# Delta-rule decays from rows of running sums instead of products with a triangle

## The reference, cut to what matters

```python
gc = jnp.cumsum(g, axis=-1)
diff = gc[..., :, None] - gc[..., None, :]
decay = masked_exp(causal, diff)
a_mat = jnp.where(strict, einsum('bhnid,bhnjd->bhnij', kb, k) * decay, 0.0)
attn = jnp.einsum('bhnid,bhnjd->bhnij', q, k) * decay
...
mu = jnp.mean(o, axis=-1, keepdims=True)
var = jnp.mean(jnp.square(o - mu), axis=-1, keepdims=True)
o = (o - mu) * lax.rsqrt(var + EPS)
```

## Time and profile before

| what | value |
| --- | --- |
| median of 3 runs (lowest to highest) | 2910.33 us (2908.55 to 2910.94) |
| profiled execution, its span | 2911.19 us, 2909.4 us |
| mean granted clock of TensorE | 0.997 |
| TensorE busy | 2861.8 us, 98% of the span |
| VectorE, ScalarE, GpSimd busy | 2027.7 us (70%), 1557.9 us (54%), 418.4 us (14%) |
| chain that ended last | TensorE 63%, issue 27%, VectorE 5%, ScalarE 2%, DMA 1% |
| a slot's load of 512 KB, issue to landing | 4.0 us |

### The profile page before, as it was taken

One profiled execution on the slowest core, in us unless ns is written; L12 is line 12 of the kernel. 1 busy time (PEld: TensorE's weight loads), 2 busy tenths in 40 slices (PEclk: granted clock), 3 DMA queues, 4 the chain that ended last, 5 costly groups with the idle time before them and its releaser, 6 DMA issues.

```text
span 2909.4 us, 44265 instructions
## 1 busy us (share of the span) xinstructions
PE 2861.8 (98%) x16572; PEld 2496.3 (86%) x16572; DVE 2027.7 (70%) x3257; ACT 1557.9 (54%) x2353; POOL 418.4 (14%) x637
## 2 busy tenths in 40 slices
PE   7999999999999999999999999999999999999998
PEld 6899889988988888888888899889988888888887
DVE  6888888888875555545568888888888754555554
ACT  6566656665664444444556556655665644444443
POOL 3222132212200000000011232123211000000000
PEclk9999999999999999999999999999999999999999
DMA  6676677667766666666656766676667666666655
GB/s 162 152 178 166 175 178 176 168 172 178 179 175 198 193 193 195 192 193 187 191 129 171 179 171 171 174 181 171 174 174 177 185 192 194 195 189 196 194 181 166
DMA packets 636358, 521.41 MB, mean 179 GB/s; under 512 B 26480, under 2 KB 504496, under 8 KB 635760
## 3 DMA queue, kind: packets, MB, share of 16 engines
q1 hardware_dynamic: 612944, 483.46, 59.1%
q0 software_dynamic: 22816, 34.00, 6.8%
q10 hardware_dynamic: 384, 1.11, 0.1%
HBM read 487.02 MB, written 2.10 MB: 168 GB/s over the span
## 4 chain that ended last, share of the span: by engine, by line
PE 63%; issue 27%; DVE 5%; ACT 2%; DVEq 2%; POOL 1%; DMA 1%; ACTq 0%; POOLq 0%
PE PJ L1807 41%; PE S L1807 16%; PE RA L1807 3%; PE GB L1807 2%; DVE w_lo L1222 1%; DVE mix L1374 1%; POOL gnorm L592 0%; POOL w_lo L507 0%; DVE region L1409 0%; ACT w_lo L656 0%; DVE region L1412 0%; DVE region L1411 0%; DVEq L1413 0%; DVE region L1419 0%; DVEq L1420 0%
## 5 line engine op out<-in xcount | busy, mean ns | idle before, releaser
L1222 DVE TENSOR_TENSOR w_lo<-raw_w,w_hi 128x1024 fp32r<-128x1024 f32 (+1 forms) x912 | 1055.9, 1160 | 689.1 <-ACT w_hi L658 656.9
L658 ACT ACTIVATE w_hi<-raw_w 128x1024 fp32r<-128x1024 f32 x912 | 963.9, 1058 | 804.7 <-PE PJ L1807 358.2
L1807 PE MATMUL PJ<-h_parts,w_hi 128*128 128x256 f32 (+1 forms) x3840 | 943.7, 327 | 1.6 <-DMA w_lo<-raw_w 1.6
L1807 PE MATMUL PJ<-w_hi,h_parts 128*128 128x512 f32 x2304 | 748.9, 396 | 2.0 <-DVE h_parts L1711 2.0
L1807 PE MATMUL PJ<-h_parts,w_lo 128*128 128x256 f32 x2560 | 721.0, 282 | 0.0
L1807 PEld LDWEIGHTS PJ<-h_parts,w_hi 128*128 128x128 f32 x3840 | 641.2, 191 | 62.0 <-issue 7.9
L1807 PEld LDWEIGHTS PJ<-w_hi,h_parts 128*128 128x128 f32 x2304 | 433.6, 188 | 90.3 <-DVE h_parts L1711 2.4
L1807 PEld LDWEIGHTS PJ<-h_parts,w_lo 128*128 128x128 f32 x2560 | 488.3, 191 | 0.0
L1807 PE MATMUL PJ<-w_lo,h_parts 128*128 128x512 f32 x1152 | 449.7, 390 | 0.0
L1807 PE MATMUL S<-w_hi,h_parts 128*128 128x512 f32 x1152 | 368.4, 389 | 0.0
L1807 PEld LDWEIGHTS S<-w_hi,h_parts 128*128 128x128 f32 x1152 | 216.2, 188 | 45.0
(11 more groups left out here) (377 smaller groups left out, 3449.1 us busy)
## 6 DMA issues: line engine op xcount, KB each, us to landing
raw_w<-w_in SPq DMA_DIRECT2D x576, 512.0 KB, 4.0
raw_w<-w_in SPq DMA_DIRECT2D x512, 128.0 KB, 2.7
raw_w<-w_branch SPq DMA_DIRECT2D x128, 512.0 KB, 4.4
raw_w<-w_out SPq DMA_DIRECT2D x64, 512.0 KB, 4.3
w_lo<-raw_w POOLq DMA_DIRECT2D x112, 256.0 KB, 4.2
raw_w<-s_glu_w SPq DMA_DIRECT2D x16, 512.0 KB, 4.4
ret_decay<-c_ret POOLq DMA_DIRECT2D x16, 128.0 KB, 4.0
out<-x_tok SPq DMA_DIRECT2D x4, 512.0 KB, 4.0
```

The source lines that it names most:

```text
L658: A_(w_hi[i % RING][:, :, :], raw_w[i % RING][:, :, :], ACT.Copy).then_inc(hi_ready, 1)
L1222: TT(w_lo[i % RING][:, 0:ks, :], raw_w[i % RING][:, 0:ks, :], w_hi[i % RING][:, 0:ks, :].bitcast(f32), ALU.subtract).then_inc(raw_used[i % ...
L1807: return nc.tensor.matmul(o, w, m, start=start, stop=stop)
```

## The change

`g_wide[:, a]` is g of the block's tokens spread over 128 columns. Its product with `upto` puts the running sum `gc[j]` along the row of every partition. VectorE then makes the exponents of both forms from this row and the column `gc[i]`, which the kernel already had in `unit_cols`, clamped at 0 on the side that the mask will remove: `dec_t` gets min(row - col, 0), `dec_s` gets max(row - col, 0), negated inside ScalarE's exponential. Two products per unit stand in for five, two Exps for three (one of them over all 384 columns of `dec_t`), and five VectorE operations are new. `dec_s` is now waited for by a semaphore of its own. On VectorE `decay_logs` and `ret_normalize` come ahead of `s5_turn(0)`; on ScalarE both Exps stand where `decays_s` stood (with u = 0 where `decays_t` stood); on GpSimd the retention's power comes ahead of the masking.

```diff
-GA_N, GB_N, HA_N, RA_N, SA_N = 20, 4, 11, 3, 4
+GA_N, GB_N, HA_N, RA_N, SA_N = 20, 3, 11, 3, 4
...
-        g_later = in_work(2, P)
-        g_bc = sq[:, 2, :]
+        g_wide = in_work(2, P)
...
                     if u == 0:
...
+                    else:
+                        pool.wait_ge(r_var_ready, n1 - 1)
+                        nc.gpsimd.tensor_tensor(r_rs[:, :], r_rs[:, :], mhalf[:, 0:2], ALU.pow).then_inc(r_rs_ready, 1)
                     pool.wait_ge(dec_raised, n1)
                     nc.gpsimd.tensor_tensor(dec_t[:, 0:3:2, :], dec_t[:, 0:3:2, :],
                                             upto.unsqueeze(1).to_broadcast([P, 2, P]), ALU.mult).then_inc(dec_masked, 1)
-                    if u:
-                        pool.wait_ge(r_var_ready, n1 - 1)
-                        nc.gpsimd.tensor_tensor(r_rs[:, :], r_rs[:, :], mhalf[:, 0:2], ALU.pow).then_inc(r_rs_ready, 1)
...
                     for a in range(2):
-                        A_(g_later[:, a, :], after, ACT.Copy, scale=gate_g[:, a, ds(v, 1)])
-                    A_(g_bc, ones[:, :], ACT.Copy, scale=gate_g[:, 1, ds(v, 1)])
+                        A_(g_wide[:, a, :], ones[:, :], ACT.Copy, scale=gate_g[:, a, ds(v, 1)])
...
-                    def decays_t():
-                        act.wait_ge(gb_w, gb0 + 1)
-                        A_(dec_t[:, 0:3:2, :], GB[:, 0:2 * P].rearrange("p (a n) -> p a n", a=2), ACT.Exp).then_inc(dec_raised, 1)
-                        A_(dec_t[:, 1, :], GB[:, 2 * P:3 * P], ACT.Exp, bias=unit_cols[:, u, C_SUF0:C_SUF0 + 1]).then_inc(gb_r, 1)
-
-                    def decays_s():
-                        act.wait_ge(gb_w, gb0 + 2)
-                        A_(dec_s[:, :, :], GB[:, 0:2 * P].rearrange("p (a n) -> p a n", a=2), ACT.Exp).then_inc(gb_r, 1)
+                    def decays():
+
+                        act.wait_ge(dec_logs, n1)
+                        A_(dec_t[:, :, :], dec_t[:, :, :], ACT.Exp).then_inc(dec_raised, 1)
+                        A_(dec_s[:, :, :], dec_s[:, :, :], ACT.Exp, scale=-1.0).then_inc(dec_s_ready, 1)
...
                         ahead(5)
-                        act.wait_ge(gdn_qkv_used, n1)
-                        decays_t()
+                        decays()
                         if n == 0:
                             stage_bc()
                         ahead(6)
-                        decays_s()
                         silu_conv(1, gq2)
...
                         ahead(1)
-                        act.wait_ge(gdn_qkv_used, n1)
-                        decays_t()
                         ahead(2)
-                        decays_s()
+                        decays()
                         stage_conv(B_GK, 0)
...
+                    def decay_logs():
+
+                        dve.wait_ge(gb_w, gb0 + 1)
+                        for a in range(2):
+                            row, at = GB[:, a * P:(a + 1) * P], unit_cols[:, u, C_GC0 + a:C_GC0 + a + 1]
+                            TS(dec_t[:, 2 * a, :], row, at, 0.0, ALU.subtract, ALU.min)
+                            TS(dec_s[:, a, :], row, at, 0.0, ALU.subtract, ALU.max)
+                        TS(dec_t[:, 1, :], GB[:, P:2 * P], unit_cols[:, u, C_SUF0:C_SUF0 + 1], None, ALU.add).then_inc(
+                            gb_r, 1)
+                        dve.drain().then_inc(dec_logs, 1)
+
...
                             s5_add(1)
+                        decay_logs()
                         bounds()
...
                         ret_variance(u - 1)
+                        decay_logs()
+                        ret_normalize(u - 1)
                         dve.wait_ge(sincos_ready, n1)
                         s5_turn(0)
-                        ret_normalize(u - 1)
                         ahead(2)
...
-                    dve.wait_ge(gb_r, gb0 + 3)
+                    dve.wait_ge(dec_s_ready, n1)
...
-                    def g_decay_t():
-
-                        pe.wait_ge(cols_ready, l1)
+                    def g_rows():
+
                         pe.wait_ge(spread_ready, n1)
                         pe.wait_ge(gb_r, gb0 + 1)
                         for a in range(2):
-                            MM(GB[:, a * P:(a + 1) * P], g_later[:, a, :], upto)
-                        MM(GB[:, 2 * P:3 * P], g_bc, upto).then_inc(gb_w, 1)
-
-                    def g_decay_s():
-                        pe.wait_ge(gb_r, gb0 + 2)
-                        for a in range(2):
-                            last = MM(GB[:, a * P:(a + 1) * P], upto, g_later[:, a, :])
+                            last = MM(GB[:, a * P:(a + 1) * P], g_wide[:, a, :], upto)
                         last.then_inc(gb_w, 1)
...
                         project(5)
-                        g_decay_t()
+                        g_rows()
...
                         project(6)
-                        g_decay_s()
...
                         g_turn(u - 1)
+                        g_rows()
                         project(1)
-                        g_decay_t()
                         r_out(u - 1)
                         project(2)
                         s_bu_all()
-                        g_decay_s()
                         project(3)
```

More of the change, by code:

```diff
@@ L388, in trunk_kernel @@
         spread_ready, dec_raised, dec_masked = sem("spread_ready"), sem("dec_raised"), sem("dec_masked")
+        dec_logs, dec_s_ready = sem("dec_logs"), sem("dec_s_ready")
         conv_staged, conv_summed, conv_done = sem("conv_staged"), sem("conv_summed"), sem("conv_done")
@@ L923, in _ @@
                     act.drain().then_inc(ha_r, 1)
-                    act.wait_ge(gb_w, gb0 + 4)
+                    act.wait_ge(gb_w, gb0 + 3)
                     for a in range(2):
@@ L1524, in _ @@
                         s5_add(1)
-                    dve.wait_ge(gb_w, gb0 + 3)
+                    dve.wait_ge(gb_w, gb0 + 2)
                     TS(gnorm[:, :], GB[:, 0:4], EPS, None, ALU.add).then_inc(gb_r, 1)
@@ L1956, in g_norms @@
                         pe.wait_ge(conv_done, cv0 + 2)
-                        pe.wait_ge(gb_r, gb0 + 3)
+                        pe.wait_ge(gb_r, gb0 + 2)
                         for m, t in enumerate((gk2, gq2)):
@@ L1972, in g_values @@
                         pe.wait_ge(conv_done, cv0 + 3)
-                        pe.wait_ge(gb_r, gb0 + 4)
+                        pe.wait_ge(gb_r, gb0 + 3)
                         for a in range(2):
```

## The result

| kernel | median (lowest to highest) | ratio to before, 95% interval |
| --- | --- | --- |
| before, beside it | 2910.40 us (2908.55 to 2910.94) | |
| after | 2933.36 us (2931.77 to 2936.24) | 1.0082 (1.007 to 1.0094) |

The change makes the kernel 23 us slower. The forecast was 2916.7 with a range up to 2923, and its slowest rival stood at 2924: the sign was right, the size was not. Nearly everything that the forecast said of VectorE, ScalarE and GpSimd is in the trace; what it lacked is a loss on TensorE for which its sum had no term.

The account below looks back on a forecast made before the run. Two paths of nearly equal length, TensorE's and a chain through VectorE, were taken to bound the kernel. Terms +3.5 + 3.2 - 0.3 = +6.4 us on 2910.33 gave 2916.7 us, range 2906 to 2923.

Parts of the forecast that it names:

- TensorE's 0.70 us: Products removed per unit on TensorE, 11.2 us over 16 units; claimed to become only a wait at g_norms.
- its twin for layer 1: Layer 1, unit 0: TensorE's saving ahead of g_norms only lengthens its wait there; g_norms comes 3.15 us later.
- three signs of being wrong: No TensorE wait at g_norms, decay_logs under 1.2 us, or the mask stretching a VectorE operation.
- VectorE's part: Units with u > 0: decay_logs takes 1.41 us, path 0.25 us longer per unit, +3.5 us over 14 units.
- The hole: VectorE idle after ret_variance, before s5_turn(0), about 1.25 us in each unit with u > 0; decay_logs goes there.
- Its list of signs: Profile after: no VectorE hole, operations of 347 ns, s5_turn(0) 0.25 us later, TensorE waits about 1 us and 6 us.
- TensorE's saving: Removing g_bc's and g_decay_s's products frees 0.70 us per unit, which was to become waiting for ScalarE's square of q.
- the rival in which it arrives whole: TensorE's saving counts in full because VectorE's path is shorter than read: 11.2 us go, 2899; chance 0.14.
- ScalarE, GpSimd and the transfers: Units with u > 0: later Exps, mask and slot 6 DMA are all covered, so nothing is lost.
- the rival of a collision: GpSimd's mask meets VectorE's slot 6 split or s5_add(0): 14 x 0.54 = 7.5 us more, 2924; chance 0.12.
- The units with u = 0: Exps wait for decay_logs and delay silu_conv(1) and g_norms: +3.15 us in layer 1, 0.3 gained in layer 0.
- The rival in which decay_logs fits the hole: Five operations take about 1.1 us, 14 units give 0, only u = 0 units count: +3, 2913; chance 0.24.

Follow-up runs that it names:

- experiment 1: Changed kernel with five unread 128-column products of constants ahead of g_norms in units with u > 0: 2920.97 us.
- experiment 6: Changed kernel with three unread products of constants on TensorE behind s_bu_all in units with u > 0: 2920.90 us.
- experiment 9: Changed kernel with g_norms multiplying by all 128 columns of ones in place of one: 2919.21 us.
- experiment 12: Changed kernel with two unread products of constants ahead of g_norms in units with u > 0: 2920.93 us.
- experiment 4: Kernel before, with ScalarE making the square of q four times in units with u > 0, so TensorE waits at g_norms: 2944.03 us.
- experiment 11: Kernel before, with the square of q made four times (u > 0) and g_norms multiplying by 128 columns of ones: 2924.28 us.
- experiment 7: Kernel before, with ret_normalize moved behind ahead(3) and r_turn behind project(6): 2907.39 us.
- experiment 2: Kernel before, without the three products of g_bc and g_decay_s, Exps kept (some decays not the reference's): 2909.97 us.
- experiment 3: Changed kernel with ScalarE's two Exps behind silu_conv(1) in the two units with u = 0: 2928.36 us.
- experiment 5: Changed kernel with ret_normalize behind ahead(3), r_turn behind project(6), and with u = 0 the Exps behind silu_conv(1): 2904.51 us.
- experiment 8: Changed kernel with ret_normalize behind s5_turn(0) again, as before the change: 2921.13 us.

## Why the prediction was wrong

**Where the step failed.** It is the sentence "TensorE's 0.70 us then only lengthens its wait: it stands at g_norms for about 1 us until silu_conv(1) is done, and goes on 0.25 us later than before", and its twin for layer 1, "What TensorE saves ahead of it only lengthens that wait". Both priced a wait of TensorE at its length. The wait came as said, 1.01 to 1.33 us and 6.21 us. But behind it TensorE worked at 1.2 GHz for 3.4 us in nine units, and for 10.2 us around the long wait: nine times 1.30 us and once 3.6 us, 15.3 us that stand in no term of the sum. Shown by experiments 1, 6, 9 and 12 (same path, no drop in the units with u > 0, 12.4 to 14.2 us faster) and by experiment 4 (no change, same wait, same drop); the pair of experiments 4 and 11 shows it at equal waits. The forecast named three signs of being wrong, and none of them came: none looked at the clock. Another 1.6 us are the drop between the layers, which has no term either and comes and goes among runs.

The trace of before had a row that would have raised the question. Layer 0, unit 0, TensorE, and a window behind it:

```profile
64.67 1.05 PE L1807 MATMUL GB<-ones,work 128*128 128x1 f32 x8 [2.25 <-ACT work L786]
```

```profile
66.00:69.00 3.00, 3.00 (x21) 3.00 (x20) 1.71 (x4) 2.64 (x5) 0.19 (x1) 0.68 0.77 196
```

A longer wait, in the same place, and the clock at a mean of 0.68 behind it, in the one unit of that kernel that waits there for over 0.4 us. (It would have been a hint and no proof: in experiments 4 and 7 this unit waits 2.13 and 2.33 us and has no drop behind it.) The earlier trace rows gave a clock of 1.00, and I took it for the whole kernel, while the change was about to put this wait into 14 more units. The Trainium skill, "TensorE: Matmul & The Clock Gate", Part 1, says that the half clock is the default, which activity releases, and names two states, half and full. The trace agrees: 0.50 and 1.00 are the levels here, and values between them, as 0.86 or 0.72, are in windows that hold a change from one to the other.

**VectorE's part: right.** decay_logs took 1.39 us for 1.41 said, operations of 0.34 to 0.35 for 0.347, 0.26 apart for 0.265. The hole is filled, ret_normalize follows at once. Undisturbed units have 97.15 us, where before has 96.73 to 97.25 and, in one, 97.76; over the twelve periods that can be compared the path costs 2.8 us in experiment 1 (0.6 in layer 0 and 2.2 in layer 1), 0.23 for each, for 0.25 said. That the mean comes so close is in part luck: it is 0.11 a unit in layer 0 and 0.36 in layer 1, and nothing in unit 2, on which the forecast was worked out (97.14 us for 97.15). Its list of signs also has s5_turn(0) 0.25 us later, where its own working has 257.40 for 256.30; set to the unit's start it came 0.83 later (255.70 + 1.43).

**TensorE's saving: right in the main.** Most of it is lost in a wait (experiment 2), and the rival in which it arrives whole falls. The waits for it were in the forecast with place and length.

**ScalarE, GpSimd and the transfers: right.** Both Exps, mask and DMA are covered. The mask beside s5_turn costs nothing (0.68 us with and without), so the rival of a collision falls; the rule of the Trainium skill that the forecast named ("GPSIMD Engine Reference", section 1) agrees with the trace. The stretched L1419 of the earlier trace rows, with two SBUF operands, lay on a mask of GpSimd (1507.43 to 1508.43).

**The units with u = 0: right in kind.** In layer 1 the Exp waits 3.29 us for decay_logs, and the path grows by 3.0 us for 3.15 said; the drop behind it costs more than that. In layer 0 the gain was 1.4 us for 0.3 said, and 0.4 in experiment 1; the drops lie elsewhere there in each trace, and what they give of it is not shown.

**The rival in which decay_logs fits the hole** falls by the 1.39 us.

Without the clock the forecast's sum holds: experiments 1, 6 and 12, at 2921, still have the long drop (7.95 - 4.53 = 3.4 us in experiment 1) and the one between the layers (34.4 - 32.7 = 1.7), which leaves 2916 for 2916.7 said.

**What stays open.** Five of the 14 units after have the same wait and the same one-column products and no drop (unit 1 with 1.20 us of waiting, unit 7 with 1.19, against unit 6 with 1.07 and a drop), and other units drop in experiments 3 and 4. What decides in a single unit was not settled. One-column products are not needed where the wait is longer: between the layers 128-column products follow a wait of 2.98 or 2.99 us in every trace, and nine of the 14 have a drop there, five none; in experiment 9 the wait of 6.2 us keeps a drop of 6.8 us. Nor was it tried whether one-column products without a wait, more of them than here, would do the same; the eight records of g_norms without a wait, as in most units of before, have no drop.

## What to carry to other kernels

Before taking work from an engine that is nearly always busy, see in the chain of waits whether a second path of equal length runs beside it; if so the saving becomes idle time, and both must be shortened together, as experiment 5 did by moving one small operation on two engines. Idle time of TensorE isn't to be priced at its length: look at the granted clock window by window behind the waits that the kernel already has, above all where products of few columns follow them. If a wait of about a microsecond can't be removed, put wide work behind it, move it to where wide work follows, or fill a part of it with products nobody reads; each took all the drops of the units with u > 0 away.

## What the runs showed of the hardware that was not expected

- A wait of 1.01 to 1.33 us, followed by products of one column for 0.92 us, was enough, in nine of 14 units, for a fall to 1.2 GHz that lasted 3.4 us and began 1.0 to 2.3 us after work had resumed. It cost 1.3 us (after) to 1.5 us (experiment 4).
- Waits of 0.90 to 1.21 us with 128-column products and a projection behind them (experiment 8), of 1.02 to 1.20 and 1.32 to 1.69 us ahead of wide norm products (experiments 9 and 11), and of 0.16 to 0.75 us ahead of the same one-column products (experiments 5, 6 and 12), had no fall in any unit with u > 0.
- A wait of 2.98 or 2.99 us between the layers, the same in all 14 traces, went with drops of 3.4 us in six of them, 6.8 us in three and none in five, with 128-column products behind it. A drop of 3.4 us there cost some 1.6 us, one of 6.8 some 2.7.
- The eight matmul records of g_norms need 0.92 us with one column and 1.00 us with 128 (experiment 9). Narrow products save almost nothing here, and behind a wait they cost the clock.
- More work on TensorE made the kernel 12 us faster (experiments 1, 6 and 12).
